# Gate tables of an expert layer as one single-pass product of 256 columns per token, and the top-16 rounds written out

## What is computed

```python
qp = (xt @ w_q).reshape(T, PEER_HEADS, PEER_DKEY)                 # T = 256 tokens, 8 heads
s1, s2 = scores of the two halves against 128 keys each
v1, i1 = lax.top_k(s1, 16);  v2, i2 = lax.top_k(s2, 16)
cand = v1[..., :, None] + v2[..., None, :]
vals, flat = lax.top_k(cand.reshape(T, 8, 256), 16)
experts = e1 * 128 + e2            # e1, e2: the two indices behind flat
gates = softmax(vals)
hid = gelu(einsum('cd,chkd->chk', xc, u_tab[ec]))
out = einsum('chk,chkd->cd', gc * hid, v_tab[ec])                 # 128 picks of 16384 experts for each token
```

## Time and profile before

| | us |
|---|---|
| median of 3 executions | 2315.85 |
| lowest, highest | 2314.83, 2316.34 |
| the profiled execution, its own time | 2314.72 |
| its span from the first to the last instruction | 2312.7 |
| PE busy in it | 2278.0 (98%) |
| DVE busy | 1684.5 (73%) |
| ACT busy | 1214.2 (53%) |
| POOL busy | 476.6 (21%) |

### The profile page before, as it was taken

One profiled execution on the slowest core, in us unless ns is written; L12 is line 12 of the kernel. 1 busy time (PEld: TensorE's weight loads), 2 busy tenths in 40 slices (PEclk: granted clock), 3 DMA queues, 4 the chain that ended last, 5 costly groups with the idle time before them and its releaser, 6 DMA issues.

```text
span 2312.7 us, 36297 instructions
## 1 busy us (share of the span) xinstructions
PE 2278.0 (98%) x13406; PEld 2072.4 (90%) x13406; DVE 1684.5 (73%) x2065; ACT 1214.2 (53%) x1138; POOL 476.6 (21%) x430
## 2 busy tenths in 40 slices
PE   7999999999999999999999999999999999999997
PEld 6888888888888889999999999999999999899997
DVE  5544776565655555989889989897688888888765
ACT  5534555555454344666666666565544444444443
POOL 0001342100000000243344422222222322222000
PEclk9999999999999999999999999999999999999999
DMA  7756555545456656666666899998999999999882
GB/s 279 276 192 216 207 204 209 196 164 174 166 201 222 225 199 234 211 226 228 222 235 229 318 343 336 326 331 317 356 383 366 377 382 376 370 397 379 327 305 83
DMA packets 122281, 623.70 MB, mean 270 GB/s; under 512 B 12000, under 2 KB 40928, under 8 KB 61776
## 3 DMA queue, kind: packets, MB, share of 16 engines
q1 hardware_dynamic: 58752, 423.65, 49.8%
q0 software_dynamic: 25616, 156.65, 17.9%
q10 hardware_dynamic: 37824, 42.18, 5.1%
HBM read 576.29 MB, written 46.14 MB: 269 GB/s over the span
## 4 chain that ended last, share of the span: by engine, by line
PE 79%; DVE 12%; issue 6%; ACT 1%; DMA 1%; DVEq 0%; POOL 0%; ACTq 0%; SPq 0%; POOLq 0%
PE psum L1304 17%; PE psum L947 10%; PE psum L949 10%; PE psum L948 10%; PE psum L1255 9%; PE psum L1305 8%; PE psum L1256 4%; DVE w_lo L1392 4%; PE psum L1282 2%; PE psum L1081 1%; DVE s_now L1719 1%; PE psum L1042 1%; DMA w_raw<-in_w_units 1%; PE psum L1003 1%; DVE i_top L1705 1%
## 5 line engine op out<-in xcount | busy, mean ns | idle before, releaser
L1255 PE MATMUL psum<-h2T,w_hi 128*128 128x448 f32 x2048 | 646.0, 374 | 1.4 <-DVE w_lo L1392 1.4
L1304 PE MATMUL psum<-w_ul,w_hi 128*128 128x448 f32 x2048 | 643.2, 374 | 3.5 <-DVE w_ul L1806 3.5
L1256 PE MATMUL psum<-h2T,w_lo 128*128 128x224 f32 x2048 | 543.3, 265 | 0.0
L1305 PE MATMUL psum<-w_ul,w_lo 128*128 128x224 f32 x2048 | 541.2, 264 | 0.0
L1384 DVE TENSOR_TENSOR w_lo<-w_raw,w_hi 128x2048 fp32r<-128x2048 f32 x144 | 332.2, 2312 | 214.9 <-ACT w_hi L563 214.5
L1304 PEld LDWEIGHTS psum<-w_ul,w_hi 128*128 128x128 f32 x2048 | 384.1, 188 | 34.1 <-issue 4.2
L563 ACT ACTIVATE w_hi<-w_raw 128x2048 fp32r<-128x2048 f32 x144 | 275.5, 1913 | 264.1 <-DMA w_raw<-in_w_units 231.6
L1255 PEld LDWEIGHTS psum<-h2T,w_hi 128*128 128x128 f32 x2048 | 383.8, 187 | 33.5 <-issue 3.7
L1305 PEld LDWEIGHTS psum<-w_ul,w_lo 128*128 128x128 f32 x2048 | 390.7, 191 | 0.0
L1256 PEld LDWEIGHTS psum<-h2T,w_lo 128*128 128x128 f32 x2048 | 390.2, 191 | 0.0
L1392 DVE TENSOR_TENSOR w_lo<-w_raw,w_hi 128x2048 fp32r<-128x2048 f32 x128 | 295.5, 2310 | 65.5 <-ACT w_hi L575 62.5
(11 more groups left out here) (334 smaller groups left out, 2815.0 us busy)
## 6 DMA issues: line engine op xcount, KB each, us to landing
w_raw<-in_w_units SPq DMA_DIRECT2D x272, 1024.0 KB
raw_x<-in_w_units SPq DMA_DIRECT2D x128, 1024.0 KB, 6.7
g_tab<-tab_scratch POOLq DMA_DIRECT2D x32, 896.0 KB, 8.5
h_in<-hid_scratch POOLq DMA_DIRECT2D x64, 448.0 KB
hid_scratch<-hst ACTq DMA_DIRECT2D x32, 448.0 KB, 4.5
tab_scratch<-gate_a ACTq DMA_DIRECT2D x14, 1024.0 KB, 7.0
proj_scratch<-evac ACTq DMA_DIRECT2D x24, 512.0 KB, 4.9
x_nat<-in_x POOLq DMA_DIRECT2D x2, 2048.0 KB, 9.3
```

The lines of the kernel that those rows point to most:

```text
L1255: pe.matmul(psum[:, k % 4, 0:2 * NU].rearrange("p (a t) -> p a t", a=2), uh, h2T[:, c, :, G:S], start=c == 0, stop=False, skip_group_check ...
L1256: ins = pe.matmul(psum[:, k % 4, NU:2 * NU], ul, h2T[:, c, 0, G:S], start=False, stop=c == KC - 1, skip_group_check=True)
L1304: pe.matmul(psum[:, c, 0:2 * NU].rearrange("p (a t) -> p a t", a=2), w_hi[:, s, o:o + P], ul, start=first, stop=False, skip_group_check=True)
L1305: return pe.matmul(psum[:, c, 0:NU], w_lo[:, s, o:o + P], ul[:, 0, :], start=False, stop=False, skip_group_check=True)
```

## The change

The gate tables. A step now covers 8 tokens (`TH`), so there are 28 half-tables (`NHALF`), one after every second unit. DVE makes the one-hot matrices of both indices in one instruction (`picked`, 2 x 8 x 128 elements, fp32r). `hot2a` now holds two versions for each token side by side: ACT scales the one-hot rows by the upper part of the gate (8 instructions of 128 columns), and POOL multiplies them by the lower part (`second_lower`, one instruction of 1024 columns). The gates are split twice, once for each half of the tokens (`gates_split`). PE multiplies 8 times 256 columns in fp32r. The two halves of the result are added outside: ACT copies the lower half to `low`, DVE adds the upper half from PSUM and `low` into `gate_a` (`table_added`). The store is issued by ACT after each second half, and DVE waits for it (`tab_st`) before it writes `gate_a` again.

The routing rounds. DVE's loop over rounds 1 to 5 is written out, the scores are read in place, and the copy `s_now` is gone.

The gathered rows. 32 instead of 27 are done in the hidden stage; five of them already in rounds 5 to 7, and the indices are made in round 4 instead of round 6. The last stage has two rows a round instead of three.

```diff
-PRE = 27
+PRE = 32
+PRE_EARLY = 5
-I_PICK0, I_TAB, I_PICK1, I_END = 6, 8, 9, 15
+I_ROWS, I_PICK0, I_TAB, I_PICK1, I_END = 4, 6, 8, 9, 15
+PRE_SLOTS = [(5, 3), (5, 7), (6, 3), (6, 7), (7, 3)] + [(I_TAB + (2 * n + 5) // 8, (2 * n + 5) % 8) for n in range(PRE - PRE_EARLY)]
+V_SLOTS = sorted([(0, 5)] + [(i, k) for i in range(1, U_IT - 1) for k in (1, 5)] + [(2, 7), (6, 7), (10, 7)])
...
 # POOL
+            def second_lower(hb):
+                pool.wait_ge(picks_done, hb + 1)
+                if hb:
+                    pool.wait_ge(tab_done, hb)
+                pool.tensor_tensor(hot2a[:, :, 1, :], picked[:, 1, :, :].bitcast(F32),
+                                   gate_lo[:, G + hb * TH:G + (hb + 1) * TH, None].to_broadcast([P, TH, PEER_NK]), ALU.mult).then_inc(hot2_done, 1)
...
 # ACT, k even: low half of the last table, then the upper part of the next; k % 4 == 1: the store
+                        act.activation(low[:, :, :], tables[:, :, 1, :], ACT.Copy).then_inc(low_out, 1)
...
+                        for j in range(TH):
+                            t = G + hb * TH + j
+                            ins = act.activation(hot2a[:, j, 0, :], picked[:, 1, j, :].bitcast(F32), ACT.Copy, scale=gate_hi[:, t:t + 1].bitcast(F32))
+                        ins.then_inc(hot2_done, 1)
...
 # PE
-                    if k % 4 == 2 and tables:
-                        table(i * 2 + (k // 4 - 2 * I_TAB))
+                    if k % 2 == 1 and tables:
+                        table(i * 4 + (k // 2 - 4 * I_TAB))
...
-                    pe.wait_ge(tab_out, 2 * (I_PICK1 - I_TAB))
+                    pe.wait_ge(tab_out, 4 * (I_PICK1 - I_TAB))
...
+                for j in range(TH):
+                    ins = pe.matmul(tables[:, j, :, :], picked[:, 0, j, :], hot2a[:, j, :, :], start=True, stop=True, skip_group_check=True)
...
 # DVE
-                        step(dve.tensor_copy(s_now[:, :, :].rearrange("p a n -> p (a n)"), sc[:, ds(u, 1), :].rearrange("p a n -> p (a n)")), alone=True)
+            def picks(hb):
+                if hb:
+                    dve.wait_ge(hot2_done, 2 * hb)
+                    dve.wait_ge(tab_done, hb)
+                dve.tensor_tensor(picked[:, :, :, :], iota[:, None, None, :].to_broadcast([P, 2, TH, PEER_NK]), ...
+            def table_added(hb):
+                dve.wait_ge(low_out, hb + 1)
+                if hb == 0:
+                    dve.wait_ge(hg_done, 1)
+                elif hb % 2 == 0:
+                    dve.wait_ge(tab_st, 16 * (hb // 2))
+                dve.tensor_tensor(staged[:, hb % 2 * TH:(hb % 2 + 1) * TH, :], tables[:, :, 0, :], low[:, :, :], ALU.add).then_inc(tab_out, 1)
```

188 lines of the change are left out of this document (94 added, 94 removed).

## The result

The changed kernel takes 2355.45 us (median of 4 runs, 2350.11 to 2359.79) against 2315.41 for the kernel before in the same session: ratio 1.0169, 95% interval 1.0157 to 1.0181. It is slower by 40 us, where the forecast was 8 us slower with a range to 2345. The profiled run is 2353.75 us, span 2352.1.

A forecast was written before the change was run, and what follows sets the result against it. PE was taken as the bound before, DVE with POOL after. Pairs +4.8, stage start +3.5, routing -3, last stage -1, store +2, handovers +1.4 gave +7.7 us: 2322.4, as median 2323.5, range 2298 to 2345.

The forecast's parts named there:

- 22 us less of work: Table rounds, PE: 48.9 us of old tables removed, 26.9 of half-tables added, so PE alone would gain 22.0 us.
- DVE and POOL exclude each other: Table rounds: POOL's sum and product cannot run beside DVE's subtractions, picks or rows, making a pair 11.98 us, +4.8 in all.
- 11.98: Forecast time in us of two units with their half-table: 8.84 on DVE, 0.94 for the sum, 2.2 for the product.
- two holds: Time DVE loses to POOL in each pair: 0.94 us for POOL's sum and 2.2 for its new product.
- The product's 2.2: Table rounds: POOL's lower product of 1024 columns holds DVE 2.2 us a pair, with DVE's addition hidden under it.
- has room ... nothing on the path: Table rounds, ACT: its work in a pair is 9.4 us of 11.98, so it delays nothing.
- The second rival: Late store: the next half's addition waits until gate_a is stored; 2335 to 2348 us, chance 0.20.
- The 9.8 us from issue to addition: Table rounds: DVE work between the store's issue and the addition awaiting it; a landing below 9.8 us costs nothing.
- Start of the stage: Beginning of the table rounds: 2 us of waiting at the second turning and 1.5 at the first table, +3.5.
- Routing rounds: DVE freed of the s_now copy, less five early rows, recovers 3 of 4 us lost there: -3.
- Last stage: Fewer gathered rows in the last stage give at most 1 us: -1.

The follow-up runs named there:

- e8: Changed kernel with table stores issued by SyncE and 14 instead of 27 gathered rows in the table rounds, 13 moved to the last stage: 2302.2 us, ratio 0.9936.
- e11: Kernel before, old tables kept, with written-out routing rounds, five early rows, 14 rows in the table rounds and 45 in the last stage: 2314.6 us, ratio 1.0000.
- e5: Changed kernel storing only the first sixteenth of each table, the last stage loading other bytes instead: 2324.7 us, ratio 1.0035.
- e13: e5 with POOL's sum in the table rounds cut to 4 columns of 224 in each half: 2302.4 us, ratio 0.9942.
- e14: e5 with POOL's lower product made over one column of 128, the sum whole: 2323.7 us, ratio 1.0034.
- e15: Changed kernel whose table stores read a buffer nobody writes, so the addition needs no wait for the store; ACT still issues: 2353.5 us, ratio 1.0160.
- e16: e15 with the table stores issued by SyncE behind the weight load instead of by ACT: 2326.2 us, ratio 1.0043.
- e7: Changed kernel with the 14 table stores issued by SyncE on the weight loads' queue instead of by ACT: 2328.0 us, ratio 1.0049.
- e9: Changed kernel with 25 of the 27 gathers of the table rounds fetching 512 bytes of a row instead of 8 KB: 2329.6 us, ratio 1.0065.
- e12: Changed kernel with half of the table rounds' gathered rows moved to the last stage, the store left with ACT: 2304.4 us, ratio 0.9952.
- e10: e8 with the first gate split and picks moved into the seventh routing round, POOL's first lower product before its last two lookups: 2302.4 us, ratio 0.9944.
- e4: Changed kernel with no table work on POOL: ACT makes the lower gate columns, DVE adds both halves by one reduction from PSUM: 2385.7 us, ratio 1.0298.

## Why the prediction was wrong, point by point

**PE: right.** 0.96 us per half-table as forecast. The 22 us less of work are real: PE is busy for 2255.3 us in e8 against 2278.0 before, and its rounds (302.6) lie 4 us above PE's own 298.5. Of them 12 to 13 reach the kernel's time (2302.2 against 2314.6 in e11, which has the old tables); the wait before the first table, that of the turning and the half clock behind them take most of the rest.

**DVE and POOL exclude each other: right as a mechanism and in size, wrong in its parts.** 11.98 was forecast, 12.00 is measured once the store is out of the way. Of the two holds the sum's is real, 0.94 forecast and 3.25 - 2.29 = 0.96 by the row of e5 and of e13. The product's 2.2 is not in the beat (e14). It runs beside the addition, which reads PSUM, and what the beat holds in its place is the addition's own 1.98 and 0.22 of waiting for ACT. I had written that the addition hides under the product; it is the product that hides under the addition. That the sum came within 0.02 of the measured beat with one wrong part in it is luck. Only behind a held issue does the product hold a subtraction, and that was not foreseen. The product is also shorter than I had it: where no subtraction stands in its way it takes 1.90 to 1.91, not 2.35. And PE waits for the addition (`gate_a`) in front of a half-table, not for `hot2a`, as I had expected. The Trainium skill, page "SBUF — State Buffer", section "Who interferes with whom", says that a DVE instruction with at most one input in SBUF, outside the modes that use both ports, doesn't contend with GpSimd; e14 and the 1.98 beside a running product agree.

**ACT "has room ... nothing on the path": this is the step that failed.** I summed ACT's busy time (9.4 of 11.98) and gave its DMA issues no time, as the trace of before shows them at 0.34 to 0.41. The change moves the table's store from 12.5 us ahead of the hidden values' store to 1.9 to 4.1 us ahead in all rounds but one, and there the second issue lasts up to 5.74. It costs 25 us in the rounds (e15 against e16). PE waits 36.8 us in e15 and 21.5 in e16, and the half clock costs 16.6 and 4.8 (half of PE's work in the stretches granted 0.50), so nearly half of the price is the clock.

**The store: priced as the wrong thing.** The second rival (chance 0.20, 2335 to 2348) had the late landing, and landings of 11 to 12 did come. But its mechanism, the wait of the addition, is worth 0 to 3 us here: e15 has no such wait, and its rounds are 0.4 us shorter. The 9.8 us from issue to addition were right, as e7 shows with landings of 10.0 and 4.2 us of waiting. I left the cause of a late landing open; e9 and e12 show that it takes the gather beside the store.

**Start of the stage: 3.5 forecast, 12.5 of waits found.** The turning waits 5.3 (2 forecast), for the addition before it; with half the rows it is 2.6 (e8), with the small store still 5.1 (e5). The first table waits 7.2 (1.5 forecast), in all versions of the new tables but e10. I had counted DVE's queue there and not POOL's backlog, timeline of POOL in the changed kernel:

```profile
1275.71 3.21 POOL L481 TENSOR_TENSOR hot<-hot,if_top 128x512 f32<-128x512 f32 x1 [4.10 <-DVE hot L1763]
1279.06 5.62 POOL L484 TENSOR_TENSOR hot<-hot 128x256 f32<-128x256 f32 x3
1284.82 0.24 POOL L486 TENSOR_TENSOR rt<-hot 128x32 f32<-128x32 f32 x1
1285.02 1.90 POOL L493 TENSOR_TENSOR hot2a<-picked,gate_lo 128x1024 fp32r<-128x1024 f32 x1
```

The last lookup takes 9.3 us beside DVE's subtractions, and the first product stands behind it until 1286.92. That is only part of the wait. ACT's upper columns, which do not stand behind it, were ready at 1284.56, so at most 2.4 of the 7.2 us are the product's alone; and in e4, without any product on POOL, PE waits 7.2 there for ACT's copies. The picks themselves end at 1282.07, 2.2 us after PE ran out of work. DVE's rows there are long beside the lookup (the picks 2.82 instead of 2.28); no run took the lookup away.

**Routing rounds: right.** The turning is at 1192.0 - 942.9 = 249.1 us from the start of the stage instead of 252.1, the 3 us forecast. **Last stage: right but for the store.** Minus 1 was forecast, plus 1.7 came, with one wait of 2.4 us at its start behind the last store and loads; in e5 and e13 it takes 648.0, 2.4 less than before.

**The clock was not in the sum at all.** In the trace of before it never fell in these rounds, so a wait of PE was priced at its length. In the changed kernel's rounds 37.8 us of waits come with 16.0 us lost to the half clock.

## What to carry to other kernels

Count a DMA issue as an instruction that can hold its engine: when a step is moved, look at what the same engine issues within some microseconds behind it, and how many short packets stand in that queue. Taking away a wait that the profile shows can gain nothing (e15), while an "issue" entry in front of an innocent-looking copy can be most of the loss; read the lines of the queue beside the idle time that they explain. And where a faster engine makes the next one the bound by 1 us, find work of that one for which another stage has room: half the rows moved to the last stage turned 40 us of loss into 11 us of gain (e12).
